# Residue order and late value tiles in the prompt attention of layer one, and another page split and copy placing, in a two-layer decoder step on one core

## The reference, cut to what matters

```python
DIL_PATTERNS = ((128, 1), (512, 4), (2048, 16))
def dilated_group(q, k, v, q_idx, window, dil, table):      # layer one
    offs = dil * jnp.arange(window // dil + 1)
    idx = q_idx[:, None] - offs[None, :]                    # keys at distance 0, dil, 2 dil, ...
    logits = einsum('bqhd,bqjhd->bqhj', q, k[:, idx]) * ATTN_SCALE + bias(offs)
    ...softmax over the valid keys, o = probs @ v[:, idx], returns o and m + log(s)
# the three groups are merged per head by their softmax denominators
def nsa_attend(...):                                        # layer two
    # compressed blocks, 16 selected blocks of 64 keys, and a window of 512 keys,
    # each with its own keys and values; the three are summed with sigmoid gates
# every layer: x = x + mixer(rmsnorm(x)); x = x + mlp(rmsnorm(x)); outputs also hold
# the caches shifted by one token (a_win*_sample, b_win_sample) and the prompt's keys and values
```

## Time and profile before

| what | us |
|---|---|
| median of three runs (1561.82 to 1566.29) | 1565.26 |
| the profiled execution, its own time | 1564.77 |
| its span, first to last instruction | 1563.0 |
| PE busy | 1483.6 (95%) |
| DVE busy | 577.5 (37%) |
| POOL busy | 399.9 (26%) |
| ACT busy | 233.6 (15%) |

### The profile page before, as it was taken

One profiled execution on the slowest core, in us unless ns is written; L12 is line 12 of the kernel. 1 busy time (PEld: TensorE's weight loads), 2 busy tenths in 40 slices (PEclk: granted clock), 3 DMA queues, 4 the chain that ended last, 5 costly groups with the idle time before them and its releaser, 6 DMA issues.

```text
span 1563.0 us, 22230 instructions
## 1 busy us (share of the span) xinstructions
PE 1483.6 (95%) x8377; PEld 1221.1 (78%) x8377; DVE 577.5 (37%) x1439; ACT 233.6 (15%) x692; POOL 399.9 (26%) x510
## 2 busy tenths in 40 slices
PE   7999999999999999999999999987879889999997
PEld 5987887778877888888888888865656558888886
DVE  3233332135553545654354554143545222221001
ACT  1000111113431000000000011033434321000001
POOL 4024221202266332234224410024344521000000
PEclk9999999998999799999999999988989979999999
DMA  9898886848979988998889736349974937999851
GB/s 304 323 319 217 229 261 235 293 174 290 324 251 300 373 311 329 358 336 311 319 329 350 242 95 203 100 152 371 369 243 150 301 115 285 388 379 347 318 188 55
DMA packets 179953, 423.47 MB, mean 271 GB/s; under 512 B 14424, under 2 KB 153768, under 8 KB 177032
## 3 DMA queue, kind: packets, MB, share of 16 engines
q1 hardware_dynamic: 145040, 324.40, 57.6%
q0 software_dynamic: 27504, 84.60, 17.4%
q10 hardware_dynamic: 7304, 13.06, 2.3%
HBM read 413.87 MB, written 192.48 MB: 388 GB/s over the span
## 4 chain that ended last, share of the span: by engine, by line
PE 83%; DMA 5%; issue 4%; DVE 4%; SPq 2%; POOL 1%; POOLq 1%; ACT 0%; DVEq 0%; ACTq 0%
PE bank L688 34%; PE bank L883 15%; PE bank L986 5%; PE bank L901 4%; PE bank L904 4%; PE bank L908 4%; PE bank L806 2%; DMA cring<-cache_b_win 2%; PE bank L795 2%; DMA cring<-cache_b_kv 1%; PE bank L1061 1%; PE bank L1046 1%; PE bank L851 1%; PE bank L817 1%; PE bank L1160 1%
## 5 line engine op out<-in xcount | busy, mean ns | idle before, releaser
L688 PE MATMUL bank<-hT,wring 128*128 128x264 f32 x2176 | 506.2, 390 | 1.3 <-DVE area L1281 1.0
L688 PEld LDWEIGHTS bank<-hT,wring 128*128 128x128 f32 x2176 | 412.0, 192 | 76.8 <-issue 8.0
L883 PE MATMUL bank<-area,wring 128*128 128x264 f32 x1024 | 234.3, 386 | 1.0 <-issue 1.0
L883 PEld LDWEIGHTS bank<-area,wring 128*128 128x128 f32 x1024 | 194.0, 190 | 34.0 <-issue 1.4
L586 POOL DMA_INDIRECT cring<-cache_b_kv,keyrow x128 | 126.7, 990 | 206.2 <-PE bank L908 176.0
L547 POOL TENSOR_TENSOR rv<-rv 128x264 f32<-128x264 f32 x30 | 24.1, 804 | 339.0 <-ACT rv L1801 337.9
L1456 DVE STREAM_TRANSPOSE cring<-cring 128x2048 f32<-128x2048 f32 x32 | 73.9, 2308 | 74.7 <-DMA cring<-cache_b_kv,keyrow 74.7
L527 POOL DMA_DIRECT2D cring<-cache_a_win x96 | 52.2, 552 | 140.8 <-PE bank L708 72.0
L391 POOL DMA_DIRECT2D cring<-cache_b_kv x114 | 62.9, 552 | 95.3 <-issue 82.5
L1486 DVE SCALAR_TENSOR_TENSOR area<-bank,rv 128x264 f32<-128x264 f32 x64 | 27.3, 427 | 139.1 <-PE bank L688 139.0
L986 PE MATMUL bank<-hT,wring 128*128 128x264 f32 (+1 forms) x336 | 78.5, 388 | 0.0
(11 more groups left out here) (294 smaller groups left out, 1799.1 us busy)
## 6 DMA issues: line engine op xcount, KB each, us to landing
a_win_sample<-cache_a_win SPq DMA_DIRECT2D x64, 2047.0 KB, 13.1
wring<-a_w_in SPq DMA_DIRECT2D x36, 1024.0 KB, 8.3
wring<-mlp_w_up SPq DMA_DIRECT2D x32, 1024.0 KB, 11.6
wring<-mlp_w_down SPq DMA_DIRECT2D x32, 1024.0 KB, 5.6
a_win_sample<-cache_a_win SPq DMA_DIRECT2D x16, 2044.0 KB, 17.7
cring<-cache_b_kv POOLq DMA_DIRECT2D x114, 128.0 KB, 5.3
cring<-cache_b_kv SPq DMA_DIRECT2D x114, 128.0 KB, 4.3
cring<-cache_a_win POOLq DMA_DIRECT2D x96, 128.0 KB, 7.1
```

Of the source, the lines that this page charges most:

```text
L688: mm = pe.matmul(bk[half][0:width, 0:R], wring[:, blk % NW, c, half * P:half * P + width], rhs[:, c, :], start=(c == 0), stop=(c == DC - 1))
L883: mm = pe.matmul(bk[half][:, 0:R], wring[:, blk % NW, c, half * P:(half + 1) * P], upT[:, f * R:(f + 1) * R], start=(f == 0), stop=(f == F ...
```

## The change

In layer one:

- Queries stand in residue order: inside each 128 the query rows are ordered by their position modulo 4 (the eviction of query tiles writes them so; masks and the one-hot bias tables follow, the latter as matmuls of 32 columns in groups of four).
- Group 0 stays dense. For groups 1 and 2 each block of 32 query rows is multiplied only with the keys of its residue: 32 (qt 0) or 64 (qt 1) keys per group, in matmuls with 32 output rows. The logits of a step are 192 or 384 wide, where they were 384 or 768.
- The bias of the two sparse groups is a small table (`bias_sparse`) that PE spreads for each head (`repeat_sparse`) and DVE masks (`mix_sparse`); POOL mixes only the dense part.
- One DVE instruction makes logits and maximum (`logits_a`), and three logit buffers let PE work two steps ahead with the scores.
- The value tiles of groups 1 and 2 come first. Their rows are stored to DRAM, as before, and read back in residue order by eight transfers on POOL (`v12_in`, 2 MB), for which the first `pv_a` waits. The last six tiles (group 0) run inside the attention (`tile_v`, `rows_v`), one ahead of the steps and five in steps 2, 6, 10, 14 and 18.
- The output transposes run in the attention (`turn_out(c)`), the last one inside the first tile of the output projection.
- The decode attention's `values_d` move to tiles 55, 56, 59, 60, 62, 64, so that all are done ahead of the attention.

In layer two queries and gates follow the same order. POOL no longer scales the bias. The page split changes, SP/POOL/ACT from 4/4/0 to 5/2/1 for keys and from 3/3/2 to 3/2/3 for values. Shift copies: 12 instead of 16 around the attention of layer one (three behind each weight block), 42 instead of 32 through its MLP and the projection of layer two, 7 instead of 12 in the merged attention.

```diff
-KEY_PAGES = (range(0, 4), range(4, 8), range(0, 0))
-VALUE_PAGES = (range(0, 3), range(3, 6), range(6, 8))
+KEY_PAGES = (range(0, 5), range(5, 7), range(7, 8))
+VALUE_PAGES = (range(0, 3), range(3, 5), range(5, 8))
+V_ORDER = (1, 2, 0)
...
+        V_TILE_AT = {4 * c - 10: c for c in range(3, DC)}
...
-                if 4 <= i < 12 or B_UP0 <= i < B_BIN:
+                if 4 <= i < 12 or B_UP0 <= i < B_BIN + 10:
                     copy_shift()
-                if i == B_AOUT + 3:
-                    for k in range(16):
-                        sp.wait_ge(S["pv_done"], 1 + 5 * k // 3)
+                if B_AOUT <= i < B_AOUT + 4:
+                    for k in range(3):
                         copy_shift()
...
-                if i < NC + 12:
+                if i < 24 and i % 3 == 1:
                     copy_shift()
...
+                if h == 2:
+                    pool.wait_ge(S["v_kept"], 32)
...
+                                pool.dma_start(V[64 * rt + 32 * g - 32:64 * rt + 32 * g, x, 1:3, :], src[:, x, :, 1, :]).then_inc(S["v12_in"], 16)
...
             def score_a(u):
...
+                pe.matmul(b[:, near:near + (qt + 1) * P], qT[q0:q0 + HD, 0, c, qt * P:(qt + 1) * P], kT[q0:q0 + HD, 0, c, 0:(qt + 1) * P], start=True, stop=True)
+                for g in range(1, NG):
+                    keys = kT[q0:q0 + HD, g, c, 0:SEQ].rearrange("p (t n r) -> p r t n", t=RT, r=4)
+                    for a in range(4):
+                        lhs, o = qT[q0:q0 + HD, g, c, qt * P + 32 * a:qt * P + 32 * a + 32], 32 * (g - 1)
...
             def pv_a(u):
...
+                if u == 0:
+                    pe.wait_ge(S["v12_in"], 16 * 8)
...
+                for j in range(n):
+                    pe.matmul(o[:, 0:HD], pt[:, j * P:(j + 1) * P], V[:, j, 0, h * HD:(h + 1) * HD], start=(j == 0), stop=False)
+                for a in range(4):
+                    mm = pe.matmul(o[32 * a:32 * a + 32, 0:HD], pt[0:64 * n, n * P + 32 * a:n * P + 32 * a + 32],
+                                   V[0:64 * n, a // 2, 1 + a % 2, h * HD:(h + 1) * HD], start=False, stop=True)
...
             for u in range(2 * H):
-                if u + 1 < 2 * H:
-                    score_a(u + 1)
-                turn_probs((u, u), [P] * (NG * (u % 2 + 1)), LG[:, u % 2, :])
+                if u + 2 < 2 * H:
...
+                    score_a(u + 2)
...
+                turn_a(u)
+                if u % 2 == 0 and u // 2 + 2 < H:
...
+                    repeat_sparse(u // 2 + 2, 0)
+                if u in V_TILE_AT:
+                    tile_v(V_TILE_AT[u])
...
                 if u:
                     pv_a(u - 1)
+                if u % 4 == 3 and u >= 7:
+                    turn_out(u // 4 - 1)
```

More of the change, by code:

```diff
@@ L694, in _, with repeat_sparse @@
             r, held = 0, None
+            def repeat_sparse(h, o):
+                a = h // 4
+                for x in range(4):
+                    mm = pe.matmul(bk[2][32 * x:32 * x + 32, o:o + 64], ident[32 * a:32 * a + 32, 32 * a:32 * a + 32], sparse[32 * a:32 * a + 32, h % 4, :],
+                                   start=True, stop=True)
+                mm.then_inc(S["rep_done"], 1)
             def scores_d(x):
@@ L723, in values_d @@
                 mm.then_inc(S["pvd_done"], 1)
-            for blk in range(36):
+            for blk in range(N_MAIN // 2):
                 pe.wait_ge(w_landed[blk % NW], 16 * (blk // NW + 1))
@@ L778, in _ @@
                         values_d(VD_AT.index(i))
-            pe.wait_ge(S["gemm_evac"], E_AOUT)
-            rows(r, held[1])
-            pe.wait_ge(S["od_ready"], 2)
-            for st in range(2):
-                mm = pe.transpose(bk[6 + st][0:HD, 0:P], od[:, st, :], ident[:, :])
-            mm.then_inc(S["od_turned"], 1)
+                    if i == 62:
+                        pe.wait_ge(S["rows_evac"], 37)
+                        repeat_sparse(0, 0)
+                        repeat_sparse(1, 64)
             def score_a(u):
@@ new lines, in tile_v @@
+            def tile_v(c):
+                i = 64 + c
+                blk, half = i // 2, i % 2
+                pe.wait_ge(w_landed[blk % NW], 16 * (blk // NW + 1))
+                if c == 2:
+                    pe.wait_ge(S["pnd_read"], 1)
+                else:
+                    pe.wait_ge(S["rows_evac"], 40 + c)
+                for x in range(DC):
+                    mm = pe.matmul(bk[5][:, 0:R], wring[:, blk % NW, x, half * P:(half + 1) * P], hT[:, x, :], start=(x == 0), stop=(x == DC - 1))
+                mm.then_inc(S["gemm_done"], 1)
@@ new lines, in rows_v @@
+            def rows_v(c):
+                pe.wait_ge(S["gemm_evac"], E_AIN + 64 + c + 1)
+                src = vtmp_n[:, c % 2, :]
+                for rt in range(RT):
+                    pe.transpose(bk[5][:, rt * P:(rt + 1) * P], src[:, rt * P:(rt + 1) * P], ident[:, :])
+                pe.transpose(bk[5][0:NB, SEQ:SEQ + P], src[:, SEQ:R], ident[:, :]).then_inc(S["rows_turned"], 1)
+            pe.wait_ge(S["bias_evac"], 10)
+            pe.wait_ge(S["gemm_evac"], E_AIN + 65)
+            score_a(0)
@@ L999, in _ @@
                     for rt in range(RT):
-                        mm = pe.transpose(bk[2][:, rt * 48:(rt + 1) * 48], gT[0:48, rt * P:(rt + 1) * P], ident[0:48, 0:48])
+                        for a in range(4):
+                            mm = pe.matmul(bk[2][32 * a:32 * a + 32, rt * 48:(rt + 1) * 48], gT[0:48, rt * P + a:(rt + 1) * P:4], ident[0:48, 0:48], start=True, stop=True)
                     mm.then_inc(S["gate_turned"], 1)
@@ L1809, in _, with row_evac @@
             std(0)
-            for r in range(48):
+            def row_evac(r, b):
                 kv, g, c = r // 24, r // 8 % 3, r % 8
-                if c == 0 and r:
+                if kv:
+                    g = V_ORDER[g]
+                rn = rown_n if r >= 40 else rown
+                if c == 0 and 0 < r < 40:
                     act.wait_ge(S["rown_stored"], 16 * (r // 8))
@@ L1916, in _ @@
             act.wait_ge(S["pool_own"], 16)
+            for i in range(NC):
+                page_loads(act, i, 2, a_landed)
             act.wait_ge(S["hidp_done"], 1)
```

376 lines of the change are left out of this document (241 added, 135 removed).

## The result

The kernel after took 1544.91 us (median of 3 runs, 1537.61 to 1548.31) against 1565.26 before: ratio 0.9875, 95% interval 0.9838 to 0.9913. It is faster, as forecast, but by 20 us and not by 53.

What follows compares the result with a forecast made beforehand. The prediction took PE to bound the kernel, busy in nearly all of the span. Its terms summed to 1563.0 - 41 (layer one) - 12 (merged attention) = 1510, plus 2.3 outside the span: about 1512 us, range 1478 to 1545.

Steps and rivals of the forecast that it cites:

- Layer one, with 41 of the 53 us: Layer one, start of tile 66 to output projection: 115 us instead of 155.9, 41 less.
- The heads, 69 us forecast: Layer one's attention: 16 heads at 4.3 us each, 69 us in all, bounds 58 and 83.
- a sign of DVE or ACT setting it: Layer one's attention: heads of 5.5 us or more (+19, 1531) would show this; counted within a rival of chance 0.11.
- The reload, 16 us forecast: Layer one, before the first `pv_a`: 12 us of waiting and 4 for half clock behind it, bounds 0 and 30.
- reload late: Rival, layer one: reload lands only after everything issued beside it drains, PE stands 17 us or more; 1526, chance 0.14.
- The rival of half clock from narrow matmuls: Layer one's attention: narrow matmuls lower the clock, wide records double; 1576 us, 0.7% slower; chance 0.07.
- forecast end of 430: End of layer one's attention: the output projection would start near 430 us.
- my 5: Layer one, entry ahead of step 0: tile 66, two scores and transposes of the decode output, 5 us.
- The front, 0: Front of layer one, bias matmuls and sparse table: together -7 to +5 us, taken as 0.
- The projection of layer two, 0 with +8 as its bound: Projection of layer two: ten copies beside its weights just fit; 0 us, bounds 0 and +8.
- The merged attention, keys, -12: Layer two, keys: half of 16.5 us of transfer waits and 8 of half clock go; -12 us, bounds -24 and +4.
- The values and the page split, 0: Layer two, values: scale matrices ready 2.1 us sooner four times, against ACT's later exp; 0 us, bounds -9 and +8.

Runs made afterwards that it cites:

- no_narrow_scores: The kernel after with the narrow score matmuls left out in all steps but the first two: 1531.69 us (one run).
- copies_later: The kernel after with the twelve copies behind a_w_out blocks 36 to 39 issued behind blocks 38 and 39, six each: 1525.67 us, ratio 0.9790.
- pool_in_sixteen: The kernel after with POOL's one addition of the causal mask issued as sixteen, one a head: 1541.76 us, ratio 0.9904.
- combined: The kernel after with twelve copies behind a_w_out blocks 38 and 39, the causal mask added in sixteen pieces, and the old page split: 1516.88 us, ratio 0.9751.
- tiles_spread: `combined` with five value tiles in steps 8 to 24 instead of 2 to 18, decode sums two steps later, copies behind blocks 37 and 38: 1521.85 us, 0.9729.
- the fillers: Eight useless wide matmuls in each of steps 22, 26 and 30, added to `combined`: 1511.85 us, 0.9665; repeated, 0.9694; added to `copies_between`, 0.9700.
- combined_again: `combined` repeated unchanged: 1519.26 us, ratio 0.9726.
- copies_between: `combined` with the twelve copies behind a_w_out blocks 37 and 38 instead of 38 and 39: 1518.32 us, ratio 0.9717.
- keys_in_a_row: The kernel after with narrow score matmuls reading keys from consecutive columns instead of every fourth: 1545.58 us (one run).
- placing_only: The kernel before with only the copies under layer two's projection and in its merged attention placed as in the kernel after: 1538.95 us, ratio 0.9851.

## Why the prediction was wrong

The sign was right, and 1544.91 lies 0.1 us inside the range, which is luck: the misses in the two layers cancel in part. Layer one, with 41 of the 53 us, gained nothing, for three steps of its sum: the heads were priced by their columns (69 us, measured 87), the reload was taken to share the transfers with the copies half evenly (16, measured 22), and no term stood for half clock (0, measured 14 with a stop). Layer two gained 24 against 12.

**The heads, 69 us forecast.** 16 x 5.45 = 87, 18 more; 5.45 a head is above my upper bound of 5.2. I scaled groups of 6 and 12 records by their columns. In the new step the groups are short, 2 or 4 records each. A dense score of 128 columns took 0.41 us where I had 0.22, one of 256 columns 0.63 for 0.50, and a lone product 0.37 for 0.20. Each group of scores or products came 0.13 to 0.19 us dearer, the four groups of turns 0.23 together, and a head has thirteen groups. The narrow ones took 1.67 of my 0.7 to 1.7: the end of 0.030 a record was the right one. `no_narrow_scores` shows that nothing else sets the pace; a head of 5.45 is near the 5.5 that I had named as a sign of DVE or ACT setting it, but there is no wait in it. What makes a short group dear was not tried: that it is the weight loads (184 to 190 ns for 128 columns in the kernel after), or the change from one kind of matmul to the next, is a guess.

**The reload, 16 us forecast.** 22: 21.1 by `copies_later` and the 0.9 that it still waited. What failed is the share of the transfers that I gave it, between an even one and none. This is the rival "reload late", to which I gave 0.14: with everything beside it in the queues it landed at 351.6, behind even the 345 at which 10 MB would have drained. The nearest row, 26 us, had said so, and I discounted it for a smaller backlog.

**The clock.** The rival of half clock from narrow matmuls got a chance of 0.07, since PE kept 1.00 before "and a dense tile comes every fourth step". Its place was right in part: 1.00 in the 71 us where tiles lie between the heads, 0.50 soon after they end (13 us behind the last tile in `pool_in_sixteen`, 24 in `combined`, and with the stop of PE in the kernel after). `tiles_spread` and the fillers point the same way. It is a likelihood and not a rule: `combined_again` and `copies_between` kept 1.00 behind the last tile, and `tiles_spread`, `copies_between` and `keys_in_a_row` lost it between tiles. What else decides stays open. Together with DVE's stop it is 58.2 - 44.3 = 13.9 us. My sum had the tiles as mere cost, and no term for the 13 steps behind the last.

**The rest** of the 43 us (472.7 against a forecast end of 430), 43 - 18 - 22 + 16 - 14 = 5, is in pieces that I left out: seven pairs of output transposes at 0.37, tiles with their rows at 4.24 instead of 4.0, and an entry of 9.7 us (319.07 to 328.8, with a wait of 1.8 for DVE and a tile of 5.28) for my 5, of which the two scores, 2 us, stand in the heads too. The pieces come to about 2 us more than the 5, so the shares are not exact.

**The front, 0.** Right: `score_a(0)` starts at 319.07, where tile 65's end and the two `values_d` put it (318.3).

**The projection of layer two, 0 with +8 as its bound.** +9.8, past the bound, 7.6 of it in waits for `b_w_in` and 1.5 in a tile at half clock behind the second (5.32 us for 3.8). I had blamed the copies; `placing_only` has them and no wait, and it is the split that brings it.

**The merged attention, keys, -12.** -25, past my lower bound of -24. I took half of the waits and of the half clock. All of both went: with the copies apart, PE no longer waits for keys, and from 1095 to 1190 it runs at 1.00. `placing_only` shows that the copies do most of it (-21.8).

**The values and the page split, 0.** -8.5, near my bound of -9; 2.3 of it came without the split. I had set ACT's later exp against the scale matrices that are ready sooner; PE waits less for the matrices, as reckoned (11.5 us before, 6.5 after), and the other side hardly shows. That the split is worth nothing in all came out as forecast by luck: this gain is spent in the projection.

## What to carry to other kernels

Price a stream of short matmul groups by the number of its groups, and not only by columns. A late transfer is priced by the nearest row that shows it in such company, and where bulk copies stand can be worth as much as the arithmetic saved: 23 us in `placing_only`, and 16 x (6.93 - 5.45) = 24 for the heads, of which nothing was left while the copies stood beside the reload. An edit that changes nothing in total can still hold a gain and a loss; look at its stages. Where PE is the bound and its work gets thinner, look at the granted clock of stretches without a wide tile, even when PE shows no pause. The best version here, `combined` with fillers (0.9665, 0.9694 and 0.9700), is 2% below the kernel after; the later start of the copies alone gives 0.9% (`copies_later`).

## What was not expected of the hardware

**Full load at half clock.** PE busy 38 of 38 us at a granted clock of 0.50. The Trainium skill ("TensorE: Matmul & The Clock Gate", section "HAM oscillation — how this bites in real kernels") puts a falling clock down to gaps in which PE idles. In this case it also fell without any gap: 38 of 38 us in `pool_in_sixteen`, 29 of 29 in `tiles_spread`. And it is not certain in one kernel: the two profiles of the combined kernel differ (0.55 and 1.00).

**DVE held by POOL.** 8.78 us for an addition of 0.21 beside POOL's 8.84, and at most 0.57 to 0.78 beside its pieces of 0.7 us. The Trainium skill says it ("SBUF — State Buffer", section "Who interferes with whom"): an instruction of DVE with two inputs in SBUF contends with one of GpSimd that reads SBUF, and the contention is an exclusive lock. The trace agrees: DVE's addition ends at 451.86, POOL's at 451.77. The new order brings one of the three additions beside POOL's long instruction, and I had not looked for it.

**Reading with a stride.** The rule of the Trainium skill on lines of 16 bytes, cited in the prediction, is borne out in part: 0.041 against 0.027 us a record at 64 columns, 0.027 against 0.021 at 32. The 0.3 us a head agree with my estimate of 5 us in all.
